# Delta-rule layer: the l2 norm inside the projections, the output norm's squares and gate inside the chunk loop, its rows inside the output projection

## What is computed

```python
proj = h @ w_in                       # q, k, v (4096 columns), z (2048), beta, a
qkv = causal_conv_silu(qkv, w_conv)
q = l2_norm(q) * 128 ** -0.5          # 8 heads of 128, over the head's 128 elements
k = l2_norm(k)                        # 8 heads
...
def step(state, xs):                  # one chunk, 16 value heads
    v_new = u_c - w_c @ state
    o = q_c @ state + attn_c @ v_new
    state = state * last_c + k_c.T @ v_new
...
o = rms_norm(o, w_norm) * silu(z)     # root of the mean square over a head's 128 elements
return o @ w_out
```

## Time and profile before

| | |
|---|---|
| median of 3 runs | 2749.5 us (2748.18 to 2754.24) |
| profiled execution | 2757.49 us, its span 2755.6 us |
| busy over the span | PE 2570.0 us (93%), DVE 1409.2 (51%), ACT 849.9 (31%), POOL 237.1 (9%) |
| mean granted TensorE clock | 0.931 of full speed |
| chain that ended last | PE 84%, DVE 9%, ACT 3% |
| projections of the delta layer | to 241 us |
| l2 norm | to 272 us |
| chunk loop | to 638 us |
| output norm and gate | to 700 us |

### The profile page before, as it was taken

How to read it: one execution, slowest core, us unless ns; L and a number is a source line. 1 busy time by engine, 2 the same in 40 slices (tenths; PEclk the granted TensorE clock), 3 DMA queues, 4 the chain that set the end, 5 groups by cost and what they waited for, 6 DMA issues and landing times.

```text
span 2755.6 us, 40042 instructions
## 1 busy us (share of the span) xinstructions
PE 2570.0 (93%) x16152; PEld 2254.5 (82%) x16152; DVE 1409.2 (51%) x1925; ACT 849.9 (31%) x1251; POOL 237.1 (9%) x186
## 2 busy tenths in 40 slices
PE   6998999888999999989997999998997788899998
PEld 6997999888999999989886888886884445688886
DVE  6676655552554443542464666766216364534433
ACT  5322443434332222322222322223223354322322
POOL 1000222220010000100100100002003100100001
PEclk9997999896999999999886999998997899899999
DMA  3222433332122222222101344543220000122221
GB/s 127 82 86 66 104 87 81 85 68 79 62 91 93 84 85 91 92 93 77 46 0 46 128 162 168 185 152 105 100 92 16 0 0 15 61 100 98 91 92 62
DMA packets 91971, 230.92 MB, mean 84 GB/s; under 512 B 59994, under 2 KB 61612, under 8 KB 67668
## 3 DMA queue, kind: packets, MB, share of 16 engines
q1 hardware_dynamic: 86320, 197.04, 22.3%
q10 hardware_dynamic: 5540, 32.30, 3.4%
HBM read 217.67 MB, written 11.64 MB: 83 GB/s over the span
## 4 chain that ended last, share of the span: by engine, by line
PE 84%; DVE 9%; ACT 3%; issue 2%; DMA 1%; DVEq 0%; ACTq 0%; POOL 0%; POOLq 0%; SPq 0%
PE ps L289 64%; PE ps L453 2%; PE ps L479 1%; PE ps L967 1%; PE ps L293 1%; PE ps L2173 1%; PE ps L950 1%; PE ps L960 1%; PE ps L2155 1%; DMA g_EC<-scr_g 1%; PE ps L1622 1%; PE ps L1623 1%; DVE a_mx L2239 1%; DVE g_tmp L1114 1%; PE ps L979 1%
## 5 line engine op out<-in xcount | busy, mean ns | idle before, releaser
L289 PE MATMUL ps<-xa_hi,whi 128*128 128x264 f32 (+1 forms) x2512 | 654.5, 320 | 44.0 <-DVE wlo L312 19.9
L289 PE MATMUL ps<-xa_lo,whi 128*128 128x264 f32 (+1 forms) x2512 | 650.3, 318 | 0.0
L289 PE MATMUL ps<-xa_hi,wlo 128*128 128x264 f32 (+1 forms) x2512 | 648.9, 318 | 0.0
L312 DVE TENSOR_TENSOR wlo<-raw,whi 128x2048 fp32r<-128x2048 f32 x161 | 370.6, 2302 | 257.7 <-ACT whi L305 257.7
L289 PEld LDWEIGHTS ps<-xa_hi,whi 128*128 128x128 f32 x2512 | 418.6, 191 | 86.1 <-issue 32.5
L305 ACT ACTIVATE whi<-raw 128x2048 fp32r<-128x2048 f32 x161 | 307.5, 1910 | 581.4 <-PE ps L289 577.0
L289 PEld LDWEIGHTS ps<-xa_hi,wlo 128*128 128x128 f32 x2512 | 417.7, 191 | 29.8
L289 PEld LDWEIGHTS ps<-xa_lo,whi 128*128 128x128 f32 x2512 | 417.7, 191 | 29.3
L289 PE MATMUL ps<-xb_hi,whi 128*128 128x264 f32 (+1 forms) x1280 | 385.3, 342 | 7.4 <-DVE xb_lo L1739 5.6
L289 PE MATMUL ps<-xb_lo,whi 128*128 128x264 f32 (+1 forms) x1280 | 386.1, 342 | 0.0
L289 PE MATMUL ps<-xb_hi,wlo 128*128 128x264 f32 (+1 forms) x1280 | 384.3, 341 | 0.0
(11 more groups left out here) (387 smaller groups left out, 2954.1 us busy)
## 6 DMA issues: line engine op xcount, KB each, us to landing
raw<-weights SPq DMA_DIRECT2D x161, 1024.0 KB, 4.9
mod_w<-weights_mod ACTq DMA_DIRECT2D x24, 1024.0 KB, 4.9
g_EC<-scr_g SPq DMA_DIRECT2D x10, 424.0 KB, 5.1
scr_z<-z_st SPq DMA_DIRECT2D x16, 264.0 KB, 4.6
g_D<-scr_g SPq DMA_DIRECT2D x10, 371.0 KB, 5.1
scr_a<-g_AT SPq DMA_DIRECT2D x10, 318.0 KB
h<-x_in ACTq DMA_DIRECT2D x4, 528.0 KB, 8.1
z_a<-scr_z SPq DMA_DIRECT2D x4, 528.0 KB, 4.9
```

Source lines behind the costliest of these rows:

```text
L289: mm = pe.matmul(ps[:, at_ + step * c + bank, 0:tn], w[:, hb.slot, k, c * P:(c + 1) * P], x[:, k, t0:t0 + tn], start=(k == 0 and n == 0), ...
L312: dve.tensor_tensor(wlo[:, hb.slot], raw[:, hb.raw_slot], whi[:, hb.slot].bitcast(F32), ALU.subtract).then_inc(S("w_lo"), 1)
```

## The change

The l2 norm's stage is gone. Its statistics, transposes and roots are taken during the first projection blocks of v: `dve_l2_stats` after block 9, transposes inside block 10, roots behind it. The row matmuls stand behind each projection tile, two heads at a time, over blocks 11 to 15, and VectorE scales each pair right after it has taken that tile out of PSUM. All sixteen one-hot columns are one small copy (`head_one`). Blocks 9 to 16 are written out rather than looped. The first differences, decays and g_A of the chunk loop move ahead of its join, and TensorE passes the join only after z blocks 0 and 1.

In the chunk loop, ScalarE squares what it has just taken out, and TensorE sums these squares in the next half (`squares`). z comes back in three loads in t = 6, 7, 8, and ScalarE takes silu of tiles 0 to 3 at the end of t = 8 and of 4 to 7 at the end of t = 9. GpSimd multiplies heads 0 to 7 by them (`pool_gated`) ahead of the last state decay, and heads 8 to 15 in the next stage. Behind the loop, VectorE multiplies each gated tile straight by its row in PSUM; the gain goes into the high and the low part. The rows of heads 8 to 15 stand behind the output projection's first four blocks.

```diff
         def pe_gdn_in(pe):
...
-            project(HALF_IN, 1)
-            with pe.Fori(HALF_IN + 1, 2 * HALF_IN) as i:
-                project(i, 0)
-                project(i, 1)
+            project(HALF_IN, 1, during=((1, KT // 2), lambda: pe_l2_rows(pe)))
+            for i in range(HALF_IN + 1, 2 * HALF_IN):
+                for s in range(2):
+                    project(i, s, between=lambda: pe_l2_tiles(pe, i, s, 0))
+                    pe_l2_tiles(pe, i, s, 1)
+
+        L2_FIRST = 4 * HALF_IN + 5
+
+        def l2_tiles(i, s, c):
+
+            slot = 4 * i + 2 * s + c - L2_FIRST
+            return range(2 * slot, 2 * slot + 2) if 0 <= slot < 8 else ()
...
+        def pe_l2_tiles(pe, i, s, c):
+            pe.wait_ge(S("head_lo"), 1)
+            pe.wait_ge(S("head_st"), 16)
+            for n in l2_tiles(i, s, c):
+                pe.wait_ge(S("head_out"), n + 1)
+                for bank, t0, tn in FULL:
+                    for part in l2_roots[1:]:
+                        mm = pe.matmul(ps[:, 4 + 2 * (n % 2) + bank, 0:tn], head_one[0:16, n:n + 1].to_broadcast([16, P]), part[0:16, t0:t0 + tn],
+                                       start=part is l2_roots[1], stop=part is l2_roots[2])
+                mm.then_inc(S("head_all"), 1)
+
+        def act_l2_roots(act):
+            act.activation(head_one[0:16, :], ident[0:16, 0:16], ACT.Copy).then_inc(S("head_st"), 16)
+            act.wait_ge(S("head_rows"), 1)
+            for to in l2_roots[:2]:
+                act.activation(cols(to[0:16], FULL), ps[0:16, 6:8, 0:T // 2], ACT.Sqrt).then_inc(S("head_rstd"), 1)
...
         def pe_gdn(pe, join):
...
+            def squares(t):
+                for x in range(2):
+                    if t < HALVES - 2:
+                        pe.wait_ge(S("g_A"), nth(t + 2, x))
+                    pe.wait_ge(S("g_sq"), nth(t, x))
+                    for q in range(4):
+                        n = SQ_AT + 4 * t + q
+                        mm = pe.matmul(ps[0:CH, 4 * x + 1, n:n + 1], g_B1[:, 4 * x + q, :], ones[:, 0:1], start=True, stop=True)
+                if t == HALVES - 1:
+                    mm.then_inc(S("head_sums"), 16)
...
                 z = t + Z_EARLY
+                if t:
+                    squares(t - 1)
...
+            pe.wait_ge(S("head_out"), 16 + 2)
+            pe.wait_ge(S("conv_x"), 32 + 2)
             kk(0)
             for n in range(Z_EARLY):
                 z_block(n)
+            join()
...
                 for x, g in groups_of(t):
                     act.wait_ge(S("g_o"), nth(t, x))
                     act.activation(qkv[:, 16 + 4 * g:20 + 4 * g, chunk_cols(t)], four_of(4 * x + 3, P), ACT.Copy).then_inc(S("g_oev"), 1)
...
+                for x, g in groups_of(t):
+                    act.wait_ge(S("g_oev"), nth(t, x))
+                    act.activation(heads4(g_B1, x, P), qkv[:, 16 + 4 * g:20 + 4 * g, chunk_cols(t)], ACT.Square).then_inc(S("g_sq"), 1)
+                for k in range(4 * (t % 8), 4 * (t % 8) + 4 if t >= 8 else 0):
+                    act.wait_ge(S("z_in"), 16 * (t - 6))
+                    act.activation(z_a[:, k, :], z_a[:, k, :], ACT.Silu).then_inc(S("two_act"), 1)
...
+        def pool_gated(pool, tiles):
+            for t in tiles:
+                pool.wait_ge(S("two_act"), t + 1)
+                pool.tensor_tensor(qkv[:, 16 + t, 0:T], qkv[:, 16 + t, 0:T], z_tile(t), ALU.mult).then_inc(S("g_gated"), 1)
...
+                if t == HALVES - 1:
+                    pool.wait_ge(S("g_sq"), nth(t - 1, 1))
+                    pool_gated(pool, range(KT))
                 for x, g in groups_of(t):
                     pool.wait_ge(S("g_o"), nth(t, x))
                     pool.tensor_tensor(g_S[:, 4 * g:4 * g + 4, :], g_S[:, 4 * g:4 * g + 4, :],
...
         def pe_gdn_out(pe):
+            def rows(tiles):
+                for n in tiles:
+                    if n >= 2:
+                        pe.wait_ge(S("gated"), n - 1)
...
+            rows(range(KT))
             for g, (hi, lo) in enumerate(((xa_hi, xa_lo), (xb_hi, xb_lo))):
                 for j in range(4):
                     pe_hb(pe, HalfBlock(HB_GDN_OUT + N_Z + 4 * g + j), hi, lo, FULL, "two_ev", 2 * KT + 8 * g + 2 * j,
                           per_k=("two_lo", KT * g + 2) if j == 0 else None)
+                    if g == 0:
+                        rows((KT + 2 * j, KT + 2 * j + 1))
...
             for j in range(4):
+                dve_down(dve, "two_ev", HalfBlock(HB_GDN_OUT + N_Z + j), j, FULL)
                 gated(KT + 2 * j)
                 gated(KT + 2 * j + 1)
                 low(KT + 2 * j)
                 low(KT + 2 * j + 1)
-                dve_down(dve, "two_ev", HalfBlock(HB_GDN_OUT + N_Z + j), j, FULL)
```

More of the change, by code:

```diff
@@ L154, in build_program @@
         head_stat = con.take("head_stat", [P, 96])
-        head_st = [con.take(f"head_st{c}", [P, 8], F32R) for c in range(2)]
+        head_one = con.take("head_one", [P, 16], F32R)
+        head_st = [head_one[:, 8 * c:8 * c + 8] for c in range(2)]
         xa_hi = at("xa_hi", [P, KT, T], SB_XA, F32R)
@@ L235, in __init__, with end, join @@
                 self.eng, self.name, self.n = eng, name, 0
[L237 removed]
+            def end(self, join=True):
                 self.eng.drain().then_inc(S("stage_" + self.name), 1)
                 self.n += 1
+                if join:
+                    self.join()
+            def join(self):
                 for other in ENGINES:
@@ L741, in dve_gdn_in, with convolved @@
                 .then_inc(S("gates_z"), 1)
-            def convolved(i, s, split=True):
+            def convolved(i, s, split=True, also=None):
                 hb = gdn_hb(i, s)
@@ L770, in dve_gdn_in, with also @@
             dve_gdn_gates_tokens(dve)
-            with dve.Fori(HALF_IN, 2 * HALF_IN - 1) as i:
-                for s in range(2):
-                    convolved(i, s)
-            for s in range(2):
-                convolved(2 * HALF_IN - 1, s, split=s == 0)
+            def also(i, s, c):
+                dve_l2_tiles(dve, i, s, c)
+                if (i, s, c) == (2 * HALF_IN - 1, 1, 1):
+                    dve_matrices(dve, 0)
+            for i in range(HALF_IN, 2 * HALF_IN):
+                for s in range(2):
+                    if (i, s) == (HALF_IN + 1, 0):
+                        dve_l2_low(dve)
+                    convolved(i, s, split=(i, s) != (2 * HALF_IN - 1, 1), also=(lambda c: also(i, s, c)) if i > HALF_IN else None)
+                    if (i, s) == (HALF_IN, 0):
+                        dve_l2_stats(dve)
         def by_chunk(x):
@@ new lines, in pairs, with per_pair, dve_matrices @@
+        def pairs(x):
+            return x.rearrange("p (m r) t -> p m r t", m=2)
+        def per_pair(x, w=CH):
+            return x.rearrange("p (m t) -> p m t", m=2)[:, :, None, :].to_broadcast([CH, 2, 2, w])
+        def dve_matrices(dve, t):
+            a = g_AT[t % 2]
+            for x, g in groups_of(t):
+                dve.wait_ge(S("g_kk"), nth(t, x))
+                dve.wait_ge(S("g_dec"), 4 * t + x + 3)
+                dve.tensor_tensor(pairs(heads4(a, x)), per_pair(ps[0:CH, 4 * x + (1 if t else 0), 0:2 * CH]), pairs(heads4(a, x)), ALU.mult)\
+                    .then_inc(S("g_A"), 1)
@@ L1337, in pe_gdn_out @@
                           per_k=("two_lo", KT * g + 2) if j == 0 else None)
-        def act_gdn_z(act):
-            for t in range(2 * N_Z):
-                act.wait_ge(S("z_in"), 16 * (4 if t < N_Z else 6))
-                z = z_a[:, t, :] if t < N_Z else z_b[:, t - N_Z, :]
-                act.activation(z, z, ACT.Silu).then_inc(S("two_act"), 1)
+                    if g == 0:
+                        rows((KT + 2 * j, KT + 2 * j + 1))
         def act_gdn_out(act):
@@ L2462, in _ @@
                 step()
-                st.end()
+                st.end(join=st.n > 0)
 def tiles_of(v):
```

246 lines of the change are left out of this document (147 added, 99 removed).

## The result

The changed kernel takes 2728.28 us (median of 5 runs, 2723.53 to 2731.22); the kernel before, on the same chip, 2754.24 (2748.18 to 2760.12). The ratio is 0.9911, 95% interval 0.9892 to 0.9929: 26 us faster, where 45 were forecast. The time lies above the range (2693 to 2719). The profiled execution took 2728.14 us with a span of 2726.3, 29.3 less than before.

What follows compares the result with a forecast made beforehand. TensorE was taken to bound the projections, with low-clock stretches at the l2 norm and behind the loop; -20.8 + 3.5 + 0.5 - 33.3 + 5.1 = -45.0 us gave 2704.5 us, 8-in-10 range 2693 to 2719.

Steps and rivals of the forecast that it cites:

- Term 1: l2 norm moved into the projections: z blocks 0 and 1 end at 277.3 instead of 298.16, -20.8 us.
- the stall: In the projections, TensorE waits for the low part of the l2 roots: 2.5 us, bounds 0 and 5.
- Term 2: Squares and sums in the chunk loop: 0.7 us a half, +3.5 us over halves 1 to 5.
- The last half: Loop's last half: silus mostly covered by the g_EC transfer, GpSimd slowing VectorE's multiply; +2.5 us, bounds 1 and 5.
- Term 3: Last outputs to the output projection's inputs: join 11.0 us later, inputs complete 17.2 after it, -33.3 us in all.
- Term 4: Output projection: rows of heads 8 to 15 between its first four blocks, 3.9 us, and a wait of 1.2; +5.1 us.
- (a): Rival: last stretch gives less through slower GpSimd products, small matmuls, last half or VectorE; 8 to 12 us, chance 0.20.
- (b): Rival: longer table changes make ScalarE hold TensorE 1.4 us longer at each of two places; 2707.3, chance 0.04.
- (d): Rival: row matmuls and one-column sums pull the projections' clock down, lengthening them by 94 us; 2798, chance 0.03.
- halves over 1.5 us longer than before: Sign that the forecast is wrong: chunk-loop halves lengthening by more than 1.5 us.
- e: Rival: a wait holds row matmuls or sums as long as before, only the z loop moves; near 2745, chance 0.02.

Runs made afterwards that it cites:

- e8: Changed kernel with each l2 row matmul issued twice, 16 behind each of eight tiles; the loop's first matmul came at 273.1 us, against 256.8 in the changed kernel.
- e2: Changed kernel without the sums of squares in the loop (two stand-in matmuls stay); t = 1 to 5 took 181.5 us, 196.6 in the changed kernel.
- e5: e2 with 12 full 264-column matmuls added before the z block of each of t = 1 to 5; these halves took 195.2 us in all.
- e4: Changed kernel with ScalarE's silus moved behind the first merge's copies of the same half; last outputs to join 2.8 us instead of 9.8, last half 32.0 against 30.7.
- c2: Changed kernel without the early wait, with one-pass sums, silus moved as in e4 and GpSimd's first products held back; 2703.52 us, ratio 0.9805 to the kernel before.
- f1: Changed kernel with 36 full 264-column matmuls, result unused, behind the first merge of t = 0 to 5; ratio 0.9953 to the kernel before.
- f2: c2 with 36 full 264-column matmuls, result unused, behind the first merge of t = 0 to 5; ratio 0.9922 to the kernel before.
- e7: Changed kernel with the output projection's first k steps put between the row matmuls; last outputs to feed-forward sums 135.4 us, 132.6 in the changed kernel.
- e3: Changed kernel with the sums of squares moved behind the first merge of the half; t = 1 to 5 took 200.1 us, last outputs at 635.2.
- e6: Changed kernel with squares as rounded fp32r, summed by 8 two-column one-pass matmuls a half; t = 1 to 5 took 186.2 us, span 2711.7.

## Why the prediction was wrong, step by step

- **Term 1, -20.8, measured -16.9.** Mechanism, place and pace of the rows were right. Two sizes were off. The 0.122 of a full matmul, of which I wrote "I take that for the rows too", left out what each of eight groups costs once, 0.38, put down to the changes between 16-row and 128-row weights: 3.0. By the Trainium skill (TensorEngine Tiling (Array Packing), Key Properties) a change of tiling mode drains the engine; e8 fits, as the cost comes once a group, but no run here shows that the drain is the cause. And the stall: 1.89 where I took 2.5, but with 1.5 at the lower clock behind it that was in no term. Those 1.5 belong to this one execution: eight other traces have the idle and not the fall. Together, 3.4, they stand inside my upper bound of 5.
- **Term 2, +3.5, measured +12.3: the step that failed most.** "TensorE eight one-column matmuls", of which "I take 0.09, 0.7 us a half", was a slip of counting that the earlier trace rows could have shown: 24 records there, and two to a matmul. The sums took 7.0 in the five halves: 3.5 of the miss. The other 5.3 came from the clock (27.3 us at 0.50, 17.1 before), since I added the sums to halves whose length I took as fixed. e2 and e5 show it: 1.4 or 1.5 us in either form turns halves of 35 and 37 into 38.4 and 40.
- **The last half, +2.5, measured +6.5** (the halves before it gained 2.4 where I had 0.5 lost). "A table load and four activations, 3.5 us, of which the transfer covers most" is wrong: they don't stand beside the transfer but in front of TensorE's queue. e4 and c2 show it. The slow multiply of g_EC beside GpSimd was right, 3.12 after and 1.11 in c2.
- **Term 3.** Up to the join +7.6 for +8.5, inputs complete 17.9 after it for 17.2: right. What failed is the frame, "only there does the output projection have all its inputs": 36 matmuls had run under the old scaling. The step from complete inputs to matmul 37, which I took as nothing, is 3.4.
- **Term 4, +5.1, measured +6.0.** Four groups at 1.33 and a stall of 0.85 (719.90, waiting for VectorE) in place of 3.9 and 1.2.
- **Rivals.** (a) had the right direction and gave at most 12, since it held neither the clock nor the cover (its parts add up to 10.2 to 12.2, not 8 to 12). (b) did not show: behind the table load at 605.59, 1.28, the silu starts at 606.88, with nothing lost. (d) did not happen, but e8 shows that it is one doubling away.
- **Range.** The bounds were those of single steps at fixed clock. No case held that each half might lengthen by more than the work that it gets, though the list of signs had it: halves over 1.5 us longer than before; they were 2.5 longer. "Faster 0.96 (all but d and e)" should be 0.95.

Open: why the clock falls in one half and not in the next, beyond that it depends on time. f1 kept it up and f2 did not, with the same 36 matmuls, and no run tells what made the difference.

## What to carry to other kernels

Where a loop has small matmuls beside waits, added work can cost more than its own time by what it does to the clock: here 1.4 us cost 3.0. Price it from a run with the work left out, not from its own rows. Before a fall of the clock is put down to what stands ahead of it, look for the same place in every other trace at hand: behind the same idle it fell in one of nine. And before a wait is credited with a stage's length, look at what already runs under it, on the engine that you are about to give a longer queue.

## What the runs showed of the hardware

- An idle TensorE of 1.89 us in the midst of full-rate projections was followed by 1.5 us lost at the lower clock in one trace (the changed kernel's, 176.87) and by none in eight others with the same idle.
- Row matmuls with 16-row weights between 128-row ones: 0.12 each, and 0.38 a group on top.
- 16 of them in a row (2.12 us) were followed by a fall of the clock in six of eight cases, 8 (1.16 us) in none of 13 traces. With 4 at a time between groups of 6 full ones it stayed at 0.50 from 650 to 660, TensorE busy all the time (e7).
- In five halves of the loop the time at 0.50 was 0.0 (f1) to 41.0 us (e3), and 17.1 and 27.3 before and after the change; kernels with the same code up to t = 7 swapped which half had more of it when they began 0.4 to 0.9 us apart.
- Eight fp32 matmuls of one column stand as 16 records and take 1.41; eight rounded ones of two columns stand as 8 and take 0.66 (e6).
- Identical code, behind the sums of the feed-forward layer, took 1953.8 to 1965.8 us in the profiled executions of 15 programs, so a single execution cannot tell a few us.
